# Residual rows in the order of the expert weights, and fifteen weight slots, in a one-core decoder step

## The reference

```
x = x + mixing(rmsnorm(x, norm_mix))        # w_in, RG-LRU and short convolution, w_out
x = x + cross_attention(rmsnorm(x, norm_xattn))   # w_q, memory keys and values, w_o
t = rmsnorm(x, norm_moe)
p_g = softmax(t @ wg + bg); g_sel = argmax(p_g)              # 4 groups
top-2 of the 4 experts of that group; weights from their logits, times p_g[g_sel]
act = silu(t @ w_gate[e]) * (t @ w_up[e]) * gate             # 16 experts, 2048 x 512
x = x + act @ w_down[e]                                       # 512 x 2048
y = rmsnorm(x, norm_final)
```

## Time and profile before

| | |
|---|---|
| median of 3 runs | 1483.22 us |
| the profiled execution's own time | 1484.51 us |
| its span, first to last instruction | 1482.8 us |
| mean granted TensorE clock | 0.989 |
| PE busy | 1427.7 us (96%) |
| POOL busy | 796.8 us (54%) |
| DVE, ACT busy | 555.9, 190.1 us |
| DMA moved | 377.07 MB |
| start of w_o's last 106.6 us piece in the chain | 862.11 us |
| first expert product | 999.24 us |
| last expert weights in the chain of waits | 1454.07 us |

### The profile page before, as it was taken

How to read it: one execution, slowest core, us unless ns; L and a number is a source line. 1 busy time by engine, 2 the same in 40 slices (tenths; PEclk the granted TensorE clock), 3 DMA queues, 4 the chain that set the end, 5 groups by cost and what they waited for, 6 DMA issues and landing times.

```text
span 1482.8 us, 25563 instructions
## 1 busy us (share of the span) xinstructions
PE 1427.7 (96%) x9308; PEld 1089.8 (73%) x9308; DVE 555.9 (37%) x1067; ACT 190.1 (13%) x392; POOL 796.8 (54%) x1453
## 2 busy tenths in 40 slices
PE   6999999999999999999999999979999999999997
PEld 6999999998889999998777799963334334344344
DVE  3546578829575342222111342151112122122123
ACT  5100321000000010003222200051000000000003
POOL 3777587979987757763444467512451440522500
PEclk8999999999999999999999999989999999999999
DMA  8344344445654444464788744747999999999993
GB/s 256 124 161 142 107 150 129 155 145 176 208 167 162 142 166 143 146 236 191 299 318 310 248 152 154 293 189 323 421 421 422 422 422 422 422 422 422 422 422 140
DMA packets 106120, 377.07 MB, mean 254 GB/s; under 512 B 12421, under 2 KB 12421, under 8 KB 76290
## 3 DMA queue, kind: packets, MB, share of 16 engines
q1 hardware_dynamic: 103778, 371.68, 65.8%
q10 hardware_dynamic: 2272, 4.42, 0.9%
HBM read 369.30 MB, written 6.77 MB: 254 GB/s over the span
## 4 chain that ended last, share of the span: by engine, by line
PE 83%; DMA 10%; DVE 3%; ACT 2%; issue 1%; SPq 1%; POOL 0%; POOLq 0%; ACTq 0%; DVEq 0%
PE ps L840 40%; PE ps L897 13%; PE ps L1184 11%; DMA tiles<-in_expert_w_up 8%; PE ps L1250 4%; PE ps L1214 3%; PE ps L966 2%; DMA tiles<-in_expert_w_down 2%; PE ps L790 1%; PE ps L1201 1%; PE ps L984 1%; PE ps L974 1%; PE ps L1005 1%; DMA A<-in_norm_final 1%; PE ps L1032 0%
## 5 line engine op out<-in xcount | busy, mean ns | idle before, releaser
L749 POOL COPY A<-A 128x16 f32 x952 | 146.1, 213 | 289.4 <-issue 289.3
L840 PE MATMUL ps<-hT,tiles 128*128 128x144 f32 x1792 | 295.3, 288 | 3.4 <-ACT A L1406 1.5
L840 PE MATMUL ps<-A,tiles 128*128 128x144 f32 x1792 | 262.0, 286 | 0.8 <-DVE A L2003 0.7
L840 PEld LDWEIGHTS ps<-hT,tiles 128*128 128x128 f32 x1792 | 251.6, 191 | 5.0 <-issue 2.6
L840 PEld LDWEIGHTS ps<-A,tiles 128*128 128x128 f32 x1792 | 237.0, 190 | 1.9 <-DVE A L2003 0.9
L702 POOL TENSOR_TENSOR tiles<-tiles 128x512 f32<-128x512 f32 x88 | 117.3, 1333 | 173.4 <-DMA tiles<-in_w_in 70.4
L840 PE MATMUL ps<-tiles 128*128 128x144 f32 x960 | 171.1, 287 | 0.0
L1184 PE MATMUL ps<-tiles,A 128*64 128x512 f32 x512 | 147.0, 601 | 13.2 <-DMA A<-in_expert_w_up 6.4
L840 PEld LDWEIGHTS ps<-tiles 128*128 128x128 f32 x960 | 140.4, 191 | 0.0
L897 PE MATMUL ps<-tiles,mT 128*128 128x256 f32 x512 | 132.9, 382 | 1.0 <-ACT kv_stage L1440 1.0
L1709 DVE COPY pair_sums<-ps 128x144 f32<-128x144 f32 x44 | 13.5, 308 | 300.4 <-PE ps L840 300.4
(11 more groups left out here) (350 smaller groups left out, 1698.6 us busy)
## 6 DMA issues: line engine op xcount, KB each, us to landing
tiles<-in_expert_w_down SPq DMA_DIRECT2D x56, 1024.0 KB, 22.4
tiles<-in_w_in SPq DMA_DIRECT2D x40, 1024.0 KB, 5.1
tiles<-in_expert_w_gate SPq DMA_DIRECT2D x32, 1024.0 KB, 22.1
tiles<-in_expert_w_up SPq DMA_DIRECT2D x32, 1024.0 KB, 22.5
A<-in_expert_w_up SPq DMA_DIRECT2D x24, 1024.0 KB, 25.2
tiles<-in_xa_w_k SPq DMA_DIRECT2D x16, 1024.0 KB, 5.1
tiles<-in_w_out SPq DMA_DIRECT2D x16, 1024.0 KB, 5.1
tiles<-in_xa_w_q SPq DMA_DIRECT2D x16, 1024.0 KB, 5.1
```

The costliest lines, as they stand in the source:

```text
L749: m = nc.gpsimd.tensor_copy(xe[:, :, at + n:at + n + 1], h_moe_or_zero[:, :, bass.ds(token, 1)])
L840: return mm(one(u + mp, x, TH), w[:, kp, mp, :], rhs, start=(first and g == 0 and kp == 0), stop=(g == 3 and kp == 1), skip_group_check=True)
```

## The change

The residual rows are put in another order from the start: block b = 4 g + k holds the rows d = 512 g + 4 p + k. So `hT` already has the order in which a tile of expert weights is loaded with (g p k), and the turns to token rows and back, their copies, `h_moe` and `h_tok` fall away. In exchange:

- w_in, w_q and the router weights are loaded with rows in that order (router weights in eight transfers for two);
- the input x and the norm gains are turned with every fourth column (`fourths`); `pack` has 16 transposes for 8, and `vec` 8 more columns per block;
- the columns of w_out and w_o must come out in that order, so `quarter_blocks` takes every fourth column of their tiles, on POOL and on PE;
- `scatter` takes every fourth column of `y_pair`, and the output copies read PSUM in steps;
- the root of each token is not multiplied in before the experts but after: `take_roots` (six products) brings the slots' roots to PSUM, ACT applies them in the silu, and DVE multiplies them into the gate once;
- the counts of each expert are computed after the slot numbers and roots;
- the weights have 15 slots. Tiles 0 to 14 of a pair have a slot each; tiles 15 to 23 reuse those of tiles 1 to 9, at a distance of 14. The next pair's tiles 1 to 9 come at a distance of 10 from them, the rest at 24.

```diff
-PE_EVENTS, MOE_SLOTS = 11, 14
+PE_EVENTS, MOE_SLOTS, REUSE = 11, 15, 14
...
+        def fourths(x, b):
+
+            return x.rearrange("p (g n k) -> p g k n", k=KT, n=P)[:, b // KT, b % KT, :]
...
-        def quarter_blocks(t):
-
-            w = tile_of(t).rearrange("p (kp kk) (mp mm n) -> p kk mm kp mp n", kk=2, mp=2, mm=2)
+        def quarter_blocks(name, t):
+
+            w = tile_of(t)
+            if name in ("w_out", "w_o"):
+                w = w.rearrange("p (kp kk) (n mp mm) -> p kk mm kp mp n", kk=2, mp=2, mm=2)
+            else:
+                w = w.rearrange("p (kp kk) (mp mm n) -> p kk mm kp mp n", kk=2, mp=2, mm=2)
...
         def moe_slot(m):
 
-            m %= 24
-            return m if m in (12, 13) else m % 12
+            return m % 24 if m % 24 < MOE_SLOTS else m % 24 - REUSE
+
+        def moe_uses(m):
+            return 2 if MOE_SLOTS <= moe_slot(m) + REUSE < 24 else 1
 
         def moe_lag(m):
-            return 24 if m % 12 < 2 else 12
+
+            return REUSE if m % 24 >= MOE_SLOTS else 24 - REUSE if moe_uses(m) == 2 else 24
...
-        w_in, w_out, w_q, w_k, w_v, w_o = (tiles_of(a[n][0]) for n in (
-            "w_in", "w_out", "xa_w_q", "xa_w_k", "xa_w_v", "xa_w_o"))
-        e_gate = a["expert_w_gate"][0].rearrange("e (p g k) f -> e g p k f", k=KT, p=P)
+        w_out, w_k, w_v, w_o = (tiles_of(a[n][0]) for n in ("w_out", "xa_w_k", "xa_w_v", "xa_w_o"))
+        w_in, w_q = (turned_tiles_of(a[n][0]) for n in ("w_in", "xa_w_q"))
+        e_gate = a["expert_w_gate"][0].rearrange("e (g p k) f -> e g p k f", k=KT, p=P)
...
                 elif m >= 12:
-                    after_event(sp, EVENT["h_tok_rest"] + 1)
+                    sp.wait_ge(tile_used, TILE["moe"])
...
-                        m = nc.gpsimd.tensor_copy(xe[:, :, at + n:at + n + 1], h_moe_or_zero[:, :, bass.ds(token, 1)])
+                        m = nc.gpsimd.tensor_copy(xe[:, :, at + n:at + n + 1], hT[:, :, bass.ds(token, 1)])
...
+            def take_roots(out):
+
+                for s in range(2):
+                    for c in range(3):
+                        n = own_rows[c]
+                        m = mm(out[:, s:s + 1], pick[0:n, c, C * s:C * s + C], h_rstd[0:n, c:c + 1], start=(c == 0), stop=(c == 2))
+                return m
+
+            pe.wait_ge(tokens_numbered, 1)
+            pe.wait_ge(pick_ready, 1)
+            number_slots(first_slot_sums)
+            take_roots(first_slot_roots).then_inc(unit_done, 1)
             for k in range(3):
                 n = own_rows[k]
                 m = mm(bank(u, 3)[:, 0:NE], ones[0:n, :], mask16[0:n, k, :], start=(k == 0), stop=(k == 2))
             m.then_inc(unit_done, 1)
...
-            def gate_branch(t, s, i):
-
+            def gate_branch(t, s, n, i):
+
+                act.wait_ge(slot_root_out, plus(n, i, 1))
                 after_tile(act, TILE["moe"] + t + 7, i, 24)
-                fn(silu[0:C, :], ps[0:C, 4 + s, :], ACT.Silu).then_inc(silu_ready, 1)
+                fn(silu[0:C, :], ps[0:C, 4 + s, :], ACT.Silu, scale=slot_root[0:C, s:s + 1]).then_inc(silu_ready, 1)
...
-                m = mm(ps[:, 2 * (u % 2) + n, 0:T], y_pair[:, j * P:(j + 1) * P], spread[:, :], start=True, stop=True)
+                m = mm(ps[:, 2 * (u % 2) + n, 0:T], fourths(y_pair, j), spread[:, :], start=True, stop=True)
```

More of the change, by code:

```diff
@@ L64 @@
 NX = NJ - NE
+WARM = 0
 TILE, _t = {}, 0
@@ L75 @@
                ("w_k", 3), ("mix_stat", 1), ("states", 1), ("w_k_last", 1), ("w_out", 8), ("w_q", 8),
-               ("values", 8), ("heads", 2), ("w_o", 8), ("router", 1), ("h_tok", 3), ("h_moe", 1),
-               ("places", 1), ("h_moe_rest", 1), ("final_stat", 1), ("y", 3)):
+               ("values", 8), ("heads", 2), ("w_o", 8), ("router", 1), ("logits", 1),
+               ("places", 1), ("final_stat", 1), ("y", 3)):
     UNIT[_n] = _u
@@ L472, in tokens_of_slots @@
             _, tokens = nc.values_load_multi_w_load_instructions(
-                slot_row(p, first, n), engines=[engine], min_val=0, max_val=T,
-                skip_runtime_bounds_check_because="a slot's sum over the tokens holds at most one token's number, 1 to T")
+                slot_row(p, first, n), engines=[engine], min_val=0, max_val=T - 1,
+                skip_runtime_bounds_check_because="a slot's sum over the tokens holds at most one token's number, 0 to T - 1")
             return tokens
@@ L795, in _ @@
             pe.wait_ge(pack_loaded, 16 * 16)
-            turn(UNIT["pack"], lambda b: pack[0:NROWS, b * P:(b + 1) * P], NROWS, GB)
+            u = UNIT["pack"]
+            start_unit(pe, u)
+            for b in range(GB):
+                at = b % 4 * P
+                nc.tensor.transpose(bank(u, b // 4)[:, at:at + NROWS], pack[0:NROWS, b * P:(b + 1) * P], ident[0:NROWS, 0:NROWS])
+                m = nc.tensor.transpose(bank(u, b // 4)[:, at + NROWS:at + NROWS + TURNED], fourths(pack[0:TURNED, :], b),
+                                        ident[0:TURNED, 0:TURNED])
+            m.then_inc(unit_done, 1)
             for c in range(3):
@@ L1161, in _ @@
             m.then_inc(unit_done, 1)
-            for k in range(3):
-                n = own_rows[k]
-                m = mm(bank(u, 3)[:, 0:NE], ones[0:n, :], mask16[0:n, k, :], start=(k == 0), stop=(k == 2))
-            m.then_inc(unit_done, 1)
             def number_slots(out):
@@ L1172, in number_slots @@
                 m.then_inc(unit_done, 1)
+            def take_roots(out):
[8 more added lines that the diff above has]
+            take_roots(first_slot_roots).then_inc(unit_done, 1)
+            for k in range(3):
+                n = own_rows[k]
+                m = mm(bank(u, 3)[:, 0:NE], ones[0:n, :], mask16[0:n, k, :], start=(k == 0), stop=(k == 2))
+            m.then_inc(unit_done, 1)
             BRANCH_BANK, PLACE_BANK, ACT_BANK = 4, 6, 7
@@ L1545, in slots_numbered, with roots_out @@
                 copy(slot_row(p, 0, 2 * C), sums).then_inc(slots_out, 1)
-            act.wait_ge(token_rstd_ready, 1)
-            for c in range(3):
-                tokens_out(c)
-            after_event(act, EVENT["h_moe"])
-            turned_back(0, UNIT["h_moe"])
+            def roots_out(roots):
+                copy(slot_root[0:C, :], roots).then_inc(slot_root_out, 1)
             act.wait_ge(gate_in, 2)
@@ L1629, in _ @@
                 after_event(act, EVENT["y_rest"] + c - 1 if c else EVENT["y_0"], n_loops, PE_EVENTS)
-                fn(y_nat[0:rows, c, 0:2 * TW].rearrange("p (a b) -> p a b", a=2), half(u, TW, 2)[0:rows], ACT.Copy,
+                fn(y_nat[0:rows, c, 0:2 * TW].rearrange("p (a n k) -> p a n k", a=2, k=KT),
+                   half(u, TW, 2)[0:rows].rearrange("p a (k n) -> p a n k", k=KT), ACT.Copy,
                    scale=final_rstd[0:rows, c:c + 1]).then_inc(half_free[u % 2], 1)
@@ L1654, in scaled_out @@
             def scaled_out(name, u, dst, rows):
-                gains = vec[:, :, ROWS[name]].rearrange("p (b k) -> p b k", k=4).unsqueeze(3).broadcast_to([P, 2, 4, rows])
+                gains = vec[:, :, gain_row(name)].rearrange("p (b k) -> p b k", k=4).unsqueeze(3).broadcast_to([P, 2, 4, rows])
                 tt(dst[:, 0:GB, 0:rows].rearrange("p (b k) n -> p b k n", k=4), from_banks(u, rows)[:, 0:2], gains, ALU.mult
```

181 lines of the change are left out of this document (78 added, 103 removed).

## The result

| | before | after |
|---|---|---|
| median of the runs beside each other, us | 1483.33 (4 runs, 1483.09 to 1485.98) | 1610.47 (4 runs, 1609.65 to 1611.56) |
| span of the profiled execution, us | 1482.8 | 1607.9 |

The changed kernel is 1.0853 times as long (95% interval 1.0834 to 1.0872), 127 us slower. I had forecast 1503.2 us with a range of 1479 to 1536: the sign was right, the size was not. The case that came was the rival "PE's loads pay for the step", to which I had given 0.13 and 1582 us at its far end. Its estimate was still 28 us short.

A forecast was written before the change was run, and what follows sets the result against it. PE was taken to set the end before the expert stage, DMA weight streaming within it. Terms 1.2 + 20.7 - 1.9 = +20.0 us on the 1483.2 median gave 1503.2 us, range 1479 to 1536 (8 in 10).

The forecast's parts named there:

- PE's loads pay for the step: Rival, chance 0.13: in w_out, w_o and the 96 scaled turns PE becomes slower; 1521 us at 160 ns a load, 1582 at 212.
- I take nothing: PE's 128-column loads in w_out and w_o at a 16-byte step: 0 us taken, between no cost and +91 us.
- my upper bound of 212: High end for PE's strided loads: twice the columns' 106 ns, so 212 ns, +91 us on 1024 loads.
- an ACT row on PSUM: ACT taking 2048 PSUM elements, 16 apart, in 1970 ns against 1874 in a row; used as nearest evidence for PE's loads.
- POOL's sums, +20.7: Strided weight sums in w_out and w_o: 7.99 and 7.80 us per tile, making PE wait, 10.7 + 10.0 us lost.
- The rule quoted beside this term: Trainium skill on POOL: a read stepping above 8 bytes takes about half as long again; loss near 20 us.
- Start, +1.2: Kernel start: pack's eight additional transposes on PE cost 1.2 us; more columns in the vec copy lie beside PE.
- Router to first expert, -2.9: Without the turns of hT, PE begins the experts at 996.4 instead of 999.24, 2.9 us sooner, with DVE last.
- The stream: Expert weight loading: last landing at 1452.2 against 1454.1, so -1.9 us; fifteenth slot and earlier restart eaten by the distance of 10.
- The hole at tile 26: Expert stage: tile 26 waits for the first group of down, so DMA engines run empty for some 4 us.
- The claim that the distance binds only in the first round: Expert stage: in later rounds PE gains 4 us a round on the weight stream, so slot reuse distance does not bind.
- Claimed at nothing and right: Items priced at 0 us: output copies reading PSUM 128 apart, eight router weight loads, y_pair loads, later rounds' root products.

## Why the prediction was wrong, step by step

- **"I take nothing" for PE's strided loads.** This is the step that failed, and it alone is 112 us in w_out and w_o and 10 at the start. What the runs showed in its place: a load of 128 columns 16 bytes apart takes some 323 to 330 ns and not 190, and is no longer hidden behind a product. The place, the count (1024 loads) and the point from which it decides (122.8 ns) were in the rival. By estimate a product with a strided load came to 122.8 + 63.3 x 7/4 = 233.6 ns (w_o: 186.1 ns over all products, four of seven strided), above my upper bound of 212, which would still have left 22 us of it out. The bound had no row: I doubled the 106 ns for the columns and called it the far end. Taking the same 84 ns for the rest of a load, 323 ns leaves 239 for the columns, 2.2 times the 106 and close to the 233.6. And between two bounds 91 us apart I chose by an ACT row on PSUM, which is another memory; the prediction says so itself, and should have drawn the conclusion. The one source that spoke of this memory and this step was the Trainium skill, "Advanced Engine Details and Errata", section "Memory Cachelines", and to the rival with it I gave 0.13.
- **POOL's sums, +20.7.** Wrong in size and without effect. They were 6.3 us a tile, not 7.80 (L728, with two reads and a write apart, was even shorter than in a row, 1.13 for 1.27), and PE was too slow for it to matter. Alone it would be 11.3 us, most of it by way of DVE. The rule quoted beside this term, half as long again for a read with such a step, fits neither case: 1.27 went to 1.53 us with one read apart and to 2.11 with two.
- **Start, +1.2.** Pack's turns went from 1.2 to 4.2 us; another 10.5 are the scaled turns. 2.7 were given back in the profiled execution, because PE reached w_in at the full clock (its first products follow each other at 0.12 to 0.15 us; before, at 0.24 to 0.28 for some 6 us). That can't be put down to the change: w_in to w_k takes 295.2 us here, 297.9 in the kernel before, and 295.6 to 297.7 in the other runs with the start of the changed kernel.
- **Router to first expert, -2.9.** The 2.7 us by which the places came sooner was right. Lost again: 1.7 to 2.0 us to the clock, since I took away PE's work and counted only its time, and 0.9 us to ACT, whose copy of the roots stands behind its gather and releases PE's half of PSUM. I had priced that copy nowhere. Both were mended in a run, and 27.6 us is what the forecast had (27.7).
- **The stream.** The hole at tile 26 and its time (39.5 for 40.0) were right, and so was, as far as the runs with other distances tell, that it eats the fifteenth slot; with PE starting when it did, my own sum gives 484.5 for the stage, and 485.1 was measured. The claim that the distance binds only in the first round holds too: every window of 10 us from 1217 to 1577 moves 419 to 425 GB/s.
- **Claimed at nothing and right:** the output copies (ACT L1627 1110 ns, before 1111), the router's eight loads (the router's first product follows w_o's last without a wait). The `y_pair` loads were not quite free: four products take 1.29 us in the chain for 1.17, and with the root products a pair of jobs costs PE 57.6 us for 55.7. The stream's 59.6 hides it, as said.
- **The range.** It left out the far case on purpose. With two bounds that far apart and no row of the same memory, 0.13 was too little, and 1536 cut off a case that nothing on record spoke against but a row of another memory.

## What to carry to other kernels

Before a stationary operand is read with a step, look whether two of its words still share 16 bytes of SBUF: with float32 words 8 bytes apart a 128x128 load cost nearly what it does in a row (192 to 195 ns for 190), at 16 it was some 130 ns longer, and here that was 8% of the program. If an order of rows is wanted for the transfer's sake, pair rows before quadrupling them. When work is taken off an engine in front of a critical stretch, price the clock that it kept up as well as the time it took; and when a ring gets another slot, look for the load with the shortest distance, since the hole moves there.

## What the runs showed of the hardware that I had not expected

- POOL's in-place sum with both reads and the write apart was faster than in a row: 1.13 us at 16 and 32 bytes, 1.04 at 8, 1.27 in a row. The others rose: 1.27 to 1.53 with one read apart, to 2.1 with two. I have no cause for the first.
- DVE's sums with two SBUF operands ended 0.30 to 0.32 us behind the POOL operation beside them: 0.46 us alone and up to 2.25.
- The expert stage ends 445.0 to 445.2 us after one single issue in ten kernels, while that issue itself moves by 4 us with the granted clock.
